# Block attention's step tables re-ordered, one convolution step moved, and the last unit's columns halved, in a one-core kernel of six mixer and feed-forward blocks

## The chip, the cores and the metric

The program runs on one core of a Trainium2 chip. The metric is the device time of one execution in microseconds (us), from launch to the output being written. Lower is better. Engines are named as in the profile: PE (TensorE), DVE (VectorE), ACT (ScalarE), POOL (GpSimd) and SP (SyncE, which here only issues transfers).

## The reference

A token block of 256 x 1024 in float32 passes through gated linear attention, feed-forward, a gated embedding, differential attention, feed-forward and gated embedding again, then a short convolution mixer and a block attention mixer. Only the last two and the end are touched by most of the change:

```python
# short convolution: h = h + (...)
b_gate, c_gate, xv, z = jnp.split(h @ w_in, 4, axis=-1)
u = c_gate * xv
conv = conv_w[0] * u_pad[:, 0:S] + ...            # three taps
y = b_gate * conv * jax.nn.silu(z);  return y @ w_out
# block attention, 16 heads of 64, one block of 256 keys, causal, with a distance bias
q, k, v, z = jnp.split(h @ w_in, 4, axis=-1)      # q, k normalised per head
s_own = q @ k.T - slope * own_dist                # masked above the diagonal
p = softmax(s_own);  out = p @ v
y = out * jax.nn.silu(z);  return y @ w_out
```

(The quoted lines are abridged.) In differential attention each head has two score maps, and the second, times a factor, is taken from the first before the product with v.

## The kernel before

**Units.** All weights are streamed once, in 297 units of 256 rows x 512 columns (512 KB each). A unit is fetched by SP into `raw` (a ring of four buffers), split by ACT into a rounded high part `whi` (L650) and by DVE into the rest, `wlo` (L1058; rings of eight). PE then runs 12 matmuls of 128x512 for it (L1773): two token halves, two halves of the unit's rows, and the three terms high x high, low x high, high x low. A tile is 512 output columns; most have four units. In block attention (`MB_IN` is unit 257, called M+0 here) tiles 0 to 7 are M+0 to M+31, and the output product is M+32 to M+39, which is unit 296, the last one.

**Order.** Each engine runs its own instruction list in order. What lies between the units (transposes, scores, softmax, products with v) is placed by hand in the tables `DF_ORDER` (differential attention) and `MB_ORDER` (block attention). An entry `(u, step, arg)` of PE's table is run ahead of unit M+u. ACT and DVE first split the weights up to some six units past u (`split_to`), and then run the step. SP's table says when it starts the two halves of a head's round trip: `out` writes the transposed probabilities of head `arg` to DRAM (`mb_blocks`, 192 KB), and `in` reads them back with their 32x32 blocks exchanged (`mb_pT`). Ahead of an entry at u, SP fetches all units up to M+u+9. The fetch of unit n waits until DVE has split unit n-4, whose buffer it takes:

```python
def fetch(lo, hi):
    for n in range(lo, hi):
        sp.wait_ge(sem("w_lo"), max(n - RAW + 1, 2))
        sp.dma_start(raw[:, n % RAW, :], stream[SOURCE[n]])...
```

**Block attention's steps.** `mb_T` (step `qkT`) transposes a tile of queries or keys for eight heads into banks 4 and 5, four transposes each. `mb_scores(i)` does two heads, mostly into banks 4 and 5. DVE's `mb_max(hd)` adds the bias (which frees the bank) and finds the row maximum. ACT's `mb_exp(hd)` follows. Heads 0 to 7 then go through DVE's block transpose `mb_blocks(hd)` (L1656; it writes one of two buffers, and from head 2 on waits until the `out` of head hd-2 has landed) and SP's round trip. Heads 8 to 15 are transposed by PE (`pT`, L2195). `mb_av(i)` is the product with v of heads 2i and 2i+1; for i = 1 it waits for `in` of heads 2 and 3, for i = 3 for heads 6 and 7. `mb_zn(g)` scales the gates of four heads by the softmax sums (L1666); `mb_zT(g)` transposes them into bank 4 or 5 (L2229), `mb_y(g)` multiplies them with the attention's output and frees that bank.

**Convolution.** `conv_parts(t, blk, at)` on DVE first splits the weights up to `at` + 6, then runs seven steps (L1590 to L1599), of which the sixth, `y_hi` (L1598), is what PE waits for ahead of a unit of the output product.

**End.** The last unit runs its six matmuls for the first token half, then six for the second; DVE adds each half to `h` (L1711), and SP writes it out (L573).

Of the kernel before, what the change touches and what calls it, by code (L numbers as in the profile page):

```python
# [83 lines left out]
def plan(first, tiles, steps, ends_first=False):  # L84
# [36 lines left out]
        (1, "second", 0), (8, "qkT", 0), (11, "qkT", 1), (12, "qkT", 2), (13, "scores", 0), (13, "qkT", 3),  # L121
# [7 lines left out]
        (13, "qkT", 3), (14, "scores", 0), (15, "scores", 1), (16, "tile", 3), (16, "aT", 0), (16, "scores", 2),  # L129
# [49 lines left out]
        (19, "sums", 3), (20, "max", 7), (20, "blk", 5), (21, "blk", 6), (22, "unit", 3), (25, "max", 8),  # L179
        (25, "blk", 7), (25, "max", 9), (27, "max", 10), (27, "max", 11), (29, "zn", 0), (29, "max", 12),  # L180
        (30, "max", 13), (31, "max", 14), (31, "max", 15), (31, "zn", 1), (31, "y", 0), (31, "ylo", 0),
        (31, "y", 1), (32, "zn", 2), (32, "zn", 3), (33, "ylo", 1), (33, "y", 2), (33, "ylo", 2), (34, "y", 3),
# [61 lines left out]
def build(nc, stream, x, p, cols_d, rows_d, consts_d, wgate_d, out):  # L244
    ctx = ExitStack()
    with ctx:
# [168 lines left out]
        def _(sp):  # L415
# [633 lines left out]
        def _(dve):  # L1049
# [570 lines left out]
            conv_parts(CV_IN + 7, 7, END[CV_OUT] + 1, last=True)  # L1620
# [95 lines left out]
        def _(pe):  # L1716
# [10 lines left out]
            def product(tile, lhs, signal, kt0=0, need=None, hooks=(), beside=None, part=None,  # L1727
# [10 lines left out]
                for k in range(n) if only is None else (only,):  # L1738
# [21 lines left out]
                    if turned:  # L1760
                        turned_unit(u, pair, k, kt0 + 2 * k, lhs, upper, fresh, n, inside)
                        continue
                    order = [(t, kk, i) for t in range(TT) for kk in range(2) for i in range(3)]
                    if u != UNITS - 1:
                        order.sort(key=lambda x: x[2])
                    for turn, (t, kk, i) in enumerate(order):
                        a, w = terms[i]
                        if turn == (1 if u == UNITS - 1 else 4):
# [4 lines left out]
                        last = T.matmul(bank[pair + t][:, :],  # L1773
                                        lhs[a][:, kt, t * P:(t + 1) * P],
                                        w[:, u % RING, kk * NW:(kk + 1) * NW],
                                        start=part != 1 and k == kk == i == 0,
                                        stop=part != 0 and k == n - 1 and kk == 1 and i == 2)
                        if u == UNITS - 1 and kk == 1 and i == 2:
                            last.then_inc(sem("last"), 1)
                    if u != UNITS - 1:  # L1780
                        last.then_inc(sem("w_used"), 1)
# [562 lines left out]
```

## Time and profile before

| | us |
|---|---|
| median of 3 runs (lowest, highest) | 904.68 (902.65, 905.58) |
| the profiled execution | 904.63 |
| its span, first to last instruction | 902.5 |
| PE busy | 893.9 |
| DVE busy | 654.6 |
| ACT busy | 508.1 |
| POOL busy | 55.2 |

The profiled execution's own time is 2.1 us longer than its span. Busy times are of the whole span, and a matmul's record overlaps the next one's, so PE's busy time says that it hardly ever ran dry, not how fast it was.

### The profile page before, as it was taken

To read this page: it belongs to the slowest core of one execution; us is meant where nothing else is said; L and a number is where in the kernel's file an instruction comes from. 1 tells how busy PE (TensorE), PEld (TensorE's weight loads), DVE (VectorE), ACT (ScalarE), POOL (GpSimd) and SP (SyncE) were. 2 spreads that over 40 slices of the span, in tenths; PEclk is the share of its full clock that TensorE was granted. 3 is DMA by queue.
4 is the path that set the end of the run, shared out by engine and by line. 5 is a ranking of instruction groups with operands and counts; after the bars stand their busy time and mean duration, and the time that the engine had idled before them with its cause. 6 is when DMAs were issued, how large, how long until landed. Compare 5 with 4: busy or idle time off the path is not lost.

```text
span 902.5 us, 12222 instructions
## 1 busy us (share of the span) xinstructions
PE 893.9 (99%) x4358; PEld 736.8 (82%) x4358; DVE 654.6 (73%) x995; ACT 508.1 (56%) x821; POOL 55.2 (6%) x59
## 2 busy tenths in 40 slices
PE   9999999999999999999999999999999999999998
PEld 8988888888888888778888888888888888887776
DVE  6985488777736699997787666646678898689663
ACT  6756554444444667788564444435664545486681
POOL 0001000000000003111100000000010000312000
PEclk9999999999999999999999999999999999999999
DMA  7564459777756666523487777746557775657711
GB/s 270 197 230 158 153 200 312 258 243 236 242 186 209 210 214 203 166 84 127 147 299 250 240 250 242 248 147 228 208 208 268 251 262 188 228 187 217 237 57 47
DMA packets 81197, 187.47 MB, mean 208 GB/s; under 512 B 10933, under 2 KB 36661, under 8 KB 81145
## 3 DMA queue, kind: packets, MB, share of 16 engines
q1 hardware_dynamic: 80712, 186.14, 61.8%
q8 instruction: 31, 0.51, 0.2%
q10 hardware_dynamic: 432, 0.66, 0.2%
q14 instruction: 22, 0.17, 0.1%
HBM read 171.83 MB, written 14.94 MB: 207 GB/s over the span
## 4 chain that ended last, share of the span: by engine, by line
PE 81%; DVE 10%; DMA 4%; issue 3%; ACT 2%; DVEq 0%; SPq 0%; ACTq 0%
PE bank L1773 70%; DVE wlo L1058 4%; DMA raw<-stream_dram 3%; PE bank L1800 3%; PE bank L1815 1%; PE bank L2101 1%; PE bank L2185 1%; DVE cv_prod L1557 1%; DMA cv_blocks<-cv_blk 1%; PE bank L2075 1%; ACT whi L650 1%; PE bank L2214 0%; PE bank L1858 0%; PE bank L2171 0%; DVE df_m L1463 0%
## 5 line engine op out<-in xcount | busy, mean ns | idle before, releaser
L650 ACT ACTIVATE whi<-raw 128x1024 fp32r<-128x1024 f32 x295 | 306.5, 1060 | 192.1 <-DMA raw<-stream_dram 116.5
L1058 DVE TENSOR_TENSOR wlo<-raw,whi 128x1024 fp32r<-128x1024 f32 x295 | 347.9, 1214 | 55.7 <-ACT whi L650 55.0
L1773 PE MATMUL bank<-whi,x_hi 128*128 128x512 f32 x560 | 152.5, 394 | 0.0
L1773 PE MATMUL bank<-wlo,x_hi 128*128 128x512 f32 x560 | 149.9, 389 | 0.0
L1773 PE MATMUL bank<-whi,x_lo 128*128 128x512 f32 x560 | 149.8, 389 | 0.0
L1773 PEld LDWEIGHTS bank<-wlo,x_hi 128*128 128x128 f32 x560 | 105.1, 188 | 22.2
L1773 PEld LDWEIGHTS bank<-whi,x_lo 128*128 128x128 f32 x560 | 105.1, 188 | 22.0
L1773 PEld LDWEIGHTS bank<-whi,x_hi 128*128 128x128 f32 x560 | 103.4, 188 | 21.8 <-issue 1.0
L1773 PE MATMUL bank<-whi,y_hi 128*128 128x512 f32 x400 | 109.7, 395 | 0.5 <-DVE y_hi L1598 0.3
L1773 PE MATMUL bank<-wlo,y_hi 128*128 128x512 f32 x400 | 107.6, 389 | 0.0
L1773 PE MATMUL bank<-whi,y_lo 128*128 128x512 f32 x400 | 107.6, 389 | 0.0
L1773 PEld LDWEIGHTS bank<-wlo,y_hi 128*128 128x128 f32 x400 | 75.1, 188 | 15.9
L1773 PEld LDWEIGHTS bank<-whi,y_lo 128*128 128x128 f32 x400 | 75.1, 188 | 15.9
L1773 PEld LDWEIGHTS bank<-whi,y_hi 128*128 128x128 f32 x400 | 73.5, 188 | 16.8 <-issue 1.0
L803 ACT ACTIVATE ffn_silu<-bank,rstd 128x256 f32<-128x256 f32 x44 | 18.5, 472 | 79.1 <-PE bank L1773 79.1
L1282 DVE SCALAR_TENSOR_TENSOR ffn_mid<-bank,rstd,ffn_silu 128x256 f32<-128x256 f32 x44 | 19.3, 479 | 55.4 <-ACT ffn_silu L803 55.4
L1773 PE MATMUL bank<-whi,mid_hi 128*128 128x512 f32 x176 | 47.0, 389 | 0.0
L1773 PE MATMUL bank<-wlo,mid_hi 128*128 128x512 f32 x176 | 47.0, 389 | 0.0
L1773 PE MATMUL bank<-whi,mid_lo 128*128 128x512 f32 x176 | 47.0, 389 | 0.0
L1088 DVE TENSOR_TENSOR h<-h,bank 128x512 f32<-128x512 f32 x22 | 14.1, 684 | 44.1 <-PE bank L1773 43.9
L1773 PEld LDWEIGHTS bank<-wlo,mid_hi 128*128 128x128 f32 x176 | 33.0, 188 | 6.9
L1773 PEld LDWEIGHTS bank<-whi,mid_lo 128*128 128x128 f32 x176 | 33.0, 188 | 6.9
(242 smaller groups left out, 847.8 us busy)
## 6 DMA issues: line engine op xcount, KB each, us to landing
raw<-stream_dram SPq DMA_DIRECT2D x295, 512.0 KB, 4.6
ffn_blocks<-ffn_blk SPq DMA_DIRECT2D x22, 256.0 KB, 2.0
ffn_land<-ffn_blocks SPq DMA_DIRECT2D x22, 256.0 KB, 4.0
second_blocks<-h_blk SPq DMA_DIRECT2D x8, 256.0 KB, 2.0
h_land<-second_blocks SPq DMA_DIRECT2D x8, 256.0 KB, 3.3
cv_blocks<-cv_blk SPq DMA_DIRECT2D x7, 256.0 KB, 5.6
cv_land<-cv_blocks SPq DMA_DIRECT2D x7, 256.0 KB, 2.8
h_blocks<-h_blk SPq DMA_DIRECT2D x3, 512.0 KB, 6.4
```

What stands on the lines that cost most here:

```text
L650: A(whi[:, u % RING, :], raw[:, u % RAW, :], ACT.Copy).then_inc(sem("w_hi"), 1)
L803: A(sg[:, (t - tin) % 2, k, :], bank[2 * (t % 2) + k][:, 0:256], ACT.Silu, scale=rstd[:, j, k:k + 1]).then_inc(sem("ffn_silu"), 1)
L1058: V.tensor_tensor(wlo[:, u % RING, :], raw[:, u % RAW, :], whi[:, u % RING, :].bitcast(F32), ALU.subtract).then_inc(sem("w_lo"), 1)
L1088: V.tensor_tensor(h[:, t, half * HALF:(half + 1) * HALF], h[:, t, half * HALF:(half + 1) * HALF], bank[2 * (tile % 2) + t][:, :], ALU.add) ...
L1282: V.scalar_tensor_tensor(mid[:, (t - tin) % 2, :, k, :], bank[2 * (t % 2) + k][:, 256:512].rearrange("p (k n) -> p k n", k=2), rstd[:, j, ...
L1557: last = V.scalar_tensor_tensor(cprod[:, (t - CV_IN) % 2, m, k, :], src, rstd[:, 6, k:k + 1], cact[:, (t - CV_IN) % 2, k, m, :], ALU.mult, ...
L1773: last = T.matmul(bank[pair + t][:, :], lhs[a][:, kt, t * P:(t + 1) * P], w[:, u % RING, kk * NW:(kk + 1) * NW], start=part != 1 and k == ...
L1800: last = T.matmul(bank[pair + hd // 2][:, hd % 2 * SEQ:(hd % 2 + 1) * SEQ], w[:, u % RING, kk * NW + hd * P:kk * NW + (hd + 1) * P], lhs[a ...
L1815: last = T.transpose(bank[b][:, k * SEQ + t * P:k * SEQ + (t + 1) * P], src[:, t, kt * P:(kt + 1) * P], ident)
L2075: last = T.matmul(bank[DF_S_BANKS[hd][m]][:, q * SEQ:(q + 1) * SEQ], dT[r, 0, hd, q * P:(q + 1) * P], dT[r, 1, hd, :], start=True, stop=True)
L2101: last = T.matmul(bank[b][:, q * SEQ + (hd % 2) * P:q * SEQ + (hd % 2 + 1) * P], daT[:, hd % 4, k * SEQ + q * P:k * SEQ + (q + 1) * P], dv ...
L2185: last = T.matmul(bank[MB_S_BANKS[i][m]][:, (0, P)[q]:(P, 3 * P)[q]], mT[r, 0, i, q * P:(q + 1) * P], mT[r, 1, i, 0:(q + 1) * P], start=Tr ...
```

## The change

Four things are changed. (1) Table entries of differential attention: `qkT` 2 and 3 run together ahead of `scores` 0 at +13, and ACT runs `exp` of head 1 one entry earlier. (2) In block attention's tables `max` 7, `exp` 7 and the copy of `qkT` 2 move up, `av` 2 moves from +25 to +27, `zn` 0 and 1 (and on PE `zT` 0 and 1) run together ahead of the last `scores`, 7, and SP's round trips take later places among the weights. (3) The last `conv_parts` runs ahead of one split. (4) The last unit works in three pieces: the first token half whole, then two column halves of the second one in two banks of their own, whose earlier sum is added to `h` beforehand.

```diff
+LAST = ((0, 0, NW), (1, 0, NW // 2), (1, NW // 2, NW))
...
     "sp": (
-        (12, "out", 0), (14, "in", 0), (15, "out", 1), (17, "in", 1), (17, "out", 2), (17, "out", 3), (17, "in", 2),
...
+        (14, "out", 0), (15, "out", 1), (15, "in", 0), (17, "out", 2), (17, "in", 1), (18, "out", 3), (18, "out", 4),
...
-            for half in range(2):
-                for t in range(TT):
-
-                    sp.wait_ge(sem("h_new"), 28 + 2 * half + t + 1)
-                    sp.dma_start(out[t * P:(t + 1) * P, half * HALF:(half + 1) * HALF],
-                                 h[:, t, half * HALF:(half + 1) * HALF]).then_inc(sem("out_done"), 16)
-            sp.wait_ge(sem("out_done"), 64)
+            for t in range(TT):
+                sp.wait_ge(sem("h_new"), 28 + t + 1)
+                sp.dma_start(out[t * P:(t + 1) * P, 0:HALF], h[:, t, 0:HALF]).then_inc(sem("out_done"), 16)
+            for n, (t, lo, hi) in enumerate(LAST):
+                sp.wait_ge(sem("h_new"), 30 + n + 1)
+                sp.dma_start(out[t * P:(t + 1) * P, HALF + lo:HALF + hi], h[:, t, HALF + lo:HALF + hi])\
+                    .then_inc(sem("out_done"), 16)
+            sp.wait_ge(sem("out_done"), 16 * (TT + len(LAST)))
...
-            conv_parts(CV_IN + 7, 7, END[CV_OUT] + 1, last=True)
+            conv_parts(CV_IN + 7, 7, END[CV_OUT], last=True)
...
-            for t in range(TT):
-                dve.wait_ge(sem("last"), t + 1)
-                V.tensor_tensor(h[:, t, HALF:], h[:, t, HALF:], bank[2 * ((MB_OUT + 3) % 2) + t][:, :], ALU.add)\
-                    .then_inc(sem("h_new"), 1)
+            pair = 2 * ((MB_OUT + 3) % 2)
+            dve.wait_ge(sem("w_used"), UNITS - 1)
+            V.tensor_tensor(h[:, 1, HALF:], h[:, 1, HALF:], bank[pair + 1][:, :], ALU.add).then_inc(sem("h_part"), 1)
+            dve.wait_ge(sem("h_part"), 1)
+            for n, (t, lo, hi) in enumerate(LAST):
+                b = pair if t == 0 else (pair + 2) % 4 + n - 1
+                dve.wait_ge(sem("last"), n + 1)
+                V.tensor_tensor(h[:, t, HALF + lo:HALF + hi], h[:, t, HALF + lo:HALF + hi], bank[b][:, 0:hi - lo],
+                                ALU.add).then_inc(sem("h_new"), 1)
...
+            def last_unit(u, pair, k, kt, lhs, n):
+
+                c.wait(pe, "w_lo", u + 1)
+                for m, (t, lo, hi) in enumerate(LAST):
+                    b = pair if t == 0 else (pair + 2) % 4 + m - 1
+                    if t:
+                        claim(b)
+                    for kk in range(2):
+                        for i, a, w in ((0, 0, whi), (1, 0, wlo), (2, 1, whi)):
+                            last = T.matmul(bank[b][:, 0:hi - lo], lhs[a][:, kt + kk, t * P:(t + 1) * P],
+                                            w[:, u % RING, kk * NW + lo:kk * NW + hi],
+                                            start=t == 1 and kk == i == 0, stop=kk == 1 and i == 2)
+                    last.then_inc(sem("last"), 1)
```

**SP, the round trips of heads 0 to 3.** Before, from the fetch of M+8 on (a `raw` row is one unit, an `mb_blocks` row an `out`, an `mb_pT` row an `in`):

```order
L441 DMA raw<-stream_dram 128x1024 [waits w_lo] x14
L560 DMA mb_blocks<-p_tok 128x384 [waits mb_blk]
L441 DMA raw<-stream_dram 128x1024 [waits w_lo] x2
L565 DMA mb_pT<-mb_blocks 128x4x96 [waits mb_out0]
L441 DMA raw<-stream_dram 128x1024 [waits w_lo]
L560 DMA mb_blocks<-p_tok 128x384 [waits mb_blk]
L441 DMA raw<-stream_dram 128x1024 [waits w_lo] x2
L565 DMA mb_pT<-mb_blocks 128x4x96 [waits mb_out1]
L560 DMA mb_blocks<-p_tok 128x384 [waits mb_blk] x2
L565 DMA mb_pT<-mb_blocks 128x4x96 [waits mb_out0]
L441 DMA raw<-stream_dram 128x1024 [waits w_lo]
L565 DMA mb_pT<-mb_blocks 128x4x96 [waits mb_out1]
```

The same stretch in the changed kernel:

```order
L442 DMA raw<-stream_dram 128x1024 [waits w_lo] x16
L561 DMA mb_blocks<-p_tok 128x384 [waits mb_blk]
L442 DMA raw<-stream_dram 128x1024 [waits w_lo]
L561 DMA mb_blocks<-p_tok 128x384 [waits mb_blk]
L566 DMA mb_pT<-mb_blocks 128x4x96 [waits mb_out0]
L442 DMA raw<-stream_dram 128x1024 [waits w_lo] x2
L561 DMA mb_blocks<-p_tok 128x384 [waits mb_blk]
L566 DMA mb_pT<-mb_blocks 128x4x96 [waits mb_out1]
L442 DMA raw<-stream_dram 128x1024 [waits w_lo]
L561 DMA mb_blocks<-p_tok 128x384 [waits mb_blk] x2
L442 DMA raw<-stream_dram 128x1024 [waits w_lo]
L566 DMA mb_pT<-mb_blocks 128x4x96 [waits mb_out0]
```

The `out` of head 0 now stands behind units 279 and 280 (which before followed it), and the `in` of head 2 behind the fetches of units 284 and 285, where it stood ahead of both. The next two rows of the changed list are the fetch of unit 286 and the `in` of head 3, which before stood ahead of unit 285.

**DVE, maximum of head 7.** Before, after the unit-long step on `mb_tok` (`unit` 2); the four rows from L1640 to L1648 are one head's maximum:

```order
L1446 TENSOR_TENSOR mb_tok<-mb_tok,mb_ss 128x512 x2
L1640 SCALAR_TENSOR_TENSOR mb_s<-consts,bank 128x384
L1644 TENSOR_REDUCE mb_stat<-mb_s 128x1
L1645 TENSOR_REDUCE mb_stat<-mb_s 128x1
L1648 TENSOR_SCALAR mb_stat<-mb_stat 128x2
L1058 TENSOR_TENSOR wlo<-raw,whi 128x1024
L1439 TENSOR_REDUCE mb_ss<-mb_sq 128x8 x2
L1058 TENSOR_TENSOR wlo<-raw,whi 128x1024
L1640 SCALAR_TENSOR_TENSOR mb_s<-consts,bank 128x384
```

In the changed kernel:

```order
L1448 TENSOR_TENSOR mb_tok<-mb_tok,mb_ss 128x512 x2
L1642 SCALAR_TENSOR_TENSOR mb_s<-consts,bank 128x384
L1646 TENSOR_REDUCE mb_stat<-mb_s 128x1
L1647 TENSOR_REDUCE mb_stat<-mb_s 128x1
L1650 TENSOR_SCALAR mb_stat<-mb_stat 128x2
L1642 SCALAR_TENSOR_TENSOR mb_s<-consts,bank 128x384
L1646 TENSOR_REDUCE mb_stat<-mb_s 128x1
L1647 TENSOR_REDUCE mb_stat<-mb_s 128x1
L1650 TENSOR_SCALAR mb_stat<-mb_stat 128x2
L1060 TENSOR_TENSOR wlo<-raw,whi 128x1024
L1441 TENSOR_REDUCE mb_ss<-mb_sq 128x8 x2
L1060 TENSOR_TENSOR wlo<-raw,whi 128x1024
```

Head 7's maximum now stands ahead of the splits of units 281 and 282.

**PE, ahead of M+31.** Before (L2185 scores 7, L2195 transposes of probabilities, L2214 products with v, L2229 gates):

```order
L2185 MATMUL bank<-mb_qkT 128x128 x2
L2185 MATMUL bank<-mb_qkT 128x256 x2
L2195 MATMUL bank<-consts,mb_p 128x128 x3
L2214 MATMUL bank<-mb_pT,mb_v 64x256 x2
L2214 MATMUL bank<-mb_pT,mb_v 64x128 x2
L2214 MATMUL bank<-mb_pT,mb_v 64x256 x2
L2214 MATMUL bank<-mb_pT,mb_v 64x128 x2
L2195 MATMUL bank<-consts,mb_p 128x128 x3
L2229 MATMUL bank<-consts,mb_z 128x128 x8
L2195 MATMUL bank<-consts,mb_p 128x128 x3
```

In the changed kernel:

```order
L2249 MATMUL bank<-consts,mb_z 128x128 x8
L2215 MATMUL bank<-consts,mb_p 128x128 x3
L2234 MATMUL bank<-mb_pT,mb_v 64x256 x2
L2234 MATMUL bank<-mb_pT,mb_v 64x128 x2
L2234 MATMUL bank<-mb_pT,mb_v 64x256 x2
L2234 MATMUL bank<-mb_pT,mb_v 64x128 x2
L2215 MATMUL bank<-consts,mb_p 128x128 x3
L2205 MATMUL bank<-mb_qkT 128x128 x2
L2205 MATMUL bank<-mb_qkT 128x256 x2
L2215 MATMUL bank<-consts,mb_p 128x128 x3
```

The gates' transposes and the last scores have changed places.

## Rows read from the trace of the kernel before

**Rows 1.** Page, part 1: busy time, share of the span, instructions.

```profile
PE 893.9 (99%) x4358; PEld 736.8 (82%) x4358; DVE 654.6 (73%) x995; ACT 508.1 (56%) x821; POOL 55.2 (6%) x59
```

**Rows 2.** Waits of PE: who waited for whom: us in total, times, longest.

```profile
PE bank L2229 <- DVE mb_z L1666: 1.4, 1, 1.4
...
PE bank L2171 <- ACT mb_qkT L990: 0.8, 1, 0.8
PE bank L2171 <- DVE mb_s L1640: 0.6, 1, 0.6
PE bank L1773 <- DVE y_hi L1598: 0.3, 1, 0.3
PE bank L2075 <- ACT df_qkT L885: 0.2, 1, 0.2
PE bank L2061 <- issue: 0.2, 1, 0.2
PE bank L1773 <- ACT df_p L898: 0.2, 1, 0.2
```

**Rows 3.** Timeline of PE, 828.5 to 856: start us, us, line, op, count.

```profile
829.08 0.60 PE L2171 MATMUL bank<-consts,mb_tok 128*128 128x128 f32 x4
830.25 0.66 PE L2171 MATMUL bank<-consts,mb_tok 128*128 128x128 f32 x4 [0.58 <-DVE mb_s L1640]
830.84 1.52 PE L2214 MATMUL bank<-mb_pT,mb_v 128*64 128x256 f32 x16
832.29 1.21 PE L1773 MATMUL bank<-whi,x_hi 128*128 128x512 f32 x4
...
843.68 0.93 PE L2185 MATMUL bank<-mb_qkT 64*128 64x128 f32 x8
...
854.31 0.87 PE L2214 MATMUL bank<-mb_pT,mb_v 128*64 128x256 f32 x8
```

**Rows 4.** Timeline of SP's issues, 806 to 825.

```profile
806.79 0.33 SPq L560 DMA_DIRECT2D mb_blocks<-p_tok  x1
807.16 2.37 SPq L441 DMA_DIRECT2D raw<-stream_dram  x2
...
824.15 0.43 SPq L565 DMA_DIRECT2D mb_pT<-mb_blocks  x1
```

**Rows 5.** Timeline of DVE, 810 to 850.

```profile
810.97 0.86 DVE L1656 STREAM_TRANSPOSE p_tok<-mb_p 128x384 f32<-128x384 f32 x1
...
817.06 0.56 DVE L1640 SCALAR_TENSOR_TENSOR mb_s<-consts,bank 128x384 f32<-128x384 f32 x1 [0.47 <-PE bank L2185]
...
821.77 0.87 DVE L1656 STREAM_TRANSPOSE p_tok<-mb_p 128x384 f32<-128x384 f32 x1 [1.19 <-ACT mb_p L1001]
...
828.52 1.22 DVE L1058 TENSOR_TENSOR wlo<-raw,whi 128x1024 fp32r<-128x1024 f32 x1
...
844.60 0.55 DVE L1640 SCALAR_TENSOR_TENSOR mb_s<-consts,bank 128x384 f32<-128x384 f32 x1 [3.07 <-PE bank L2185]
...
847.97 2.35 DVE L1058 TENSOR_TENSOR wlo<-raw,whi 128x1024 fp32r<-128x1024 f32 x2
```

**Rows 6.** DMA issues at 806.79, 824.15 and 831.80: count, KB, us to landing.

```profile
mb_blocks<-p_tok SPq DMA_DIRECT2D x1, 192.0 KB, 1.9
...
mb_pT<-mb_blocks SPq DMA_DIRECT2D x1, 192.0 KB, 3.9
...
mb_pT<-mb_blocks SPq DMA_DIRECT2D x1, 192.0 KB, 2.6
```

**Rows 7.** Timeline of DVE, 884 to 900, and the output's DMA issues (last row).

```profile
884.28 0.74 DVE L1681 TENSOR_TENSOR mb_oT<-bank,mb_sq 128x256 f32<-128x256 f32 x2
...
899.33 0.69 DVE L1711 TENSOR_TENSOR h<-h,bank 128x512 f32<-128x512 f32 x1 [0.67 <-PE bank L1773]
...
out<-h SPq DMA_DIRECT2D x4, 256.0 KB, 2.1
```

**Rows 8.** Timeline of PE at its start: four transposes of 128x128.

```profile
4.89 1.09 PE L1815 MATMUL bank<-consts,h 128*128 128x128 f32 x4
```

More of the change, by code:

```diff
@@ L120 @@
     "pe": (
-        (1, "second", 0), (8, "qkT", 0), (11, "qkT", 1), (12, "qkT", 2), (13, "scores", 0), (13, "qkT", 3),
+        (1, "second", 0), (8, "qkT", 0), (11, "qkT", 1), (13, "qkT", 2), (13, "qkT", 3), (13, "scores", 0),
         (13, "scores", 1), (16, "scores", 2), (16, "aT", 0), (17, "qkT", 4), (18, "aT", 1), (18, "scores", 3),
@@ L128 @@
         (4, "tile", 0), (8, "tile", 1), (9, "qkT", 0), (12, "qkT", 1), (12, "tile", 2), (12, "qkT", 2),
-        (13, "qkT", 3), (14, "scores", 0), (15, "scores", 1), (16, "tile", 3), (16, "aT", 0), (16, "scores", 2),
+        (12, "qkT", 3), (14, "scores", 0), (14, "scores", 1), (16, "tile", 3), (16, "aT", 0), (16, "scores", 2),
         (17, "qkT", 4), (17, "aT", 1), (18, "scores", 3), (18, "qkT", 5), (19, "qkT", 6), (19, "qkT", 7),
@@ L160 @@
         (11, "qkT", 0), (12, "qkT", 1), (13, "scores", 0), (13, "scores", 1), (18, "scores", 2), (19, "scores", 3),
[5 rows of a table removed]
+        (22, "qkT", 2), (22, "av", 0), (22, "av", 1), (24, "qkT", 3), (25, "scores", 4), (27, "scores", 5),
[4 rows of a table added]
     "act": (
@@ L168 @@
         (14, "exp", 1), (15, "exp", 2), (16, "tile", 3), (16, "exp", 3), (16, "exp", 4), (18, "exp", 5),
-        (20, "tile", 4), (20, "exp", 6), (22, "oT", 0), (23, "exp", 7), (23, "qkT", 2), (24, "tile", 5),
+        (20, "tile", 4), (20, "exp", 6), (20, "exp", 7), (22, "qkT", 2), (22, "oT", 0), (24, "tile", 5),
         (25, "qkT", 3), (25, "exp", 8), (26, "exp", 9), (26, "pT", 8), (27, "exp", 10), (28, "tile", 6),
-        (28, "pT", 9), (29, "oT", 1), (29, "exp", 11), (30, "pT", 10), (30, "exp", 12), (30, "pT", 11),
-        (30, "exp", 13), (31, "pT", 12), (31, "exp", 14), (31, "oT", 2), (32, "yhi", 0), (32, "pT", 13),
-        (32, "tile", 7), (32, "exp", 15), (32, "yhi", 1), (32, "pT", 14), (33, "pT", 15), (34, "yhi", 2),
+        (28, "pT", 9), (29, "oT", 1), (29, "exp", 11), (30, "pT", 10), (30, "exp", 12), (30, "exp", 13),
+        (31, "pT", 11), (31, "yhi", 0), (31, "pT", 12), (31, "oT", 2), (31, "exp", 14), (32, "pT", 13),
+        (32, "exp", 15), (32, "tile", 7), (32, "yhi", 1), (32, "pT", 14), (33, "pT", 15), (34, "yhi", 2),
         (35, "zT", 3), (36, "yhi", 3),),
@@ L178 @@
         (17, "max", 4), (17, "max", 5), (17, "blk", 3), (17, "blk", 4), (18, "unit", 2), (18, "max", 6),
[L179 to L182, printed above, removed]
+        (18, "max", 7), (19, "sums", 3), (20, "blk", 5), (21, "blk", 6), (22, "unit", 3), (25, "max", 8),
+        (25, "blk", 7), (25, "max", 9), (27, "max", 10), (27, "max", 11), (29, "zn", 0), (29, "zn", 1),
+        (29, "max", 12), (30, "max", 13), (31, "y", 0), (31, "y", 1), (31, "max", 14), (31, "max", 15),
+        (31, "ylo", 0), (32, "zn", 2), (32, "zn", 3), (33, "ylo", 1), (33, "y", 2), (33, "ylo", 2), (34, "y", 3),
         (35, "ylo", 3),),
     "sp": (
-        (12, "out", 0), (14, "in", 0), (15, "out", 1), (17, "in", 1), (17, "out", 2), (17, "out", 3), (17, "in", 2),
-        (18, "in", 3), (18, "out", 4), (19, "in", 4), (20, "out", 5), (21, "in", 5), (22, "out", 6), (23, "in", 6),
-        (23, "out", 7), (24, "in", 7),),
+        (14, "out", 0), (15, "out", 1), (15, "in", 0), (17, "out", 2), (17, "in", 1), (18, "out", 3), (18, "out", 4),
+        (19, "in", 2), (20, "in", 3), (21, "out", 5), (22, "out", 6), (23, "in", 4), (23, "in", 5), (24, "in", 6),
+        (26, "out", 7), (27, "in", 7),),
 }
@@ L1762, in product @@
                         continue
+                    if u == UNITS - 1:
+                        last_unit(u, pair, k, kt0 + 2 * k, lhs, n)
+                        continue
                     order = [(t, kk, i) for t in range(TT) for kk in range(2) for i in range(3)]
-                    if u != UNITS - 1:
-                        order.sort(key=lambda x: x[2])
+                    order.sort(key=lambda x: x[2])
                     for turn, (t, kk, i) in enumerate(order):
                         a, w = terms[i]
-                        if turn == (1 if u == UNITS - 1 else 4):
+                        if turn == 4:
                             c.wait(pe, "w_lo", u + 1)
@@ L1776, in product @@
                                         start=part != 1 and k == kk == i == 0,
[L1777 to L1781, printed above, removed]
+                                        stop=part != 0 and kk == 1 and i == 2 and (k == n - 1 or (u == UNITS - 2 and t == 1)))
+                    last.then_inc(sem("w_used"), 1)
                 if signal is not None:
```

9 rows, old and new, of the table MB_ORDER are left out of this document.

## The prediction

> **What bounds the kernel now.** I read the page's busy times first. PE is busy for 99% of the span and DVE, the next one, for 73% [rows 1], so time is won only where PE stands still and lost only where it is made to. PE's waits come next. Among them seven lie where the change works, and they sum to 1.4 + 0.8 + 0.6 + 0.3 + 0.2 + 0.2 + 0.2 = 3.7 us [rows 2]. The listed length is a little short, because a matmul's record runs on past the start of the next one. Four transposes that start at 829.08 have a record of 0.60 us, so they start some 0.11 apart and the fifth was due at about 829.52. It started at 830.25, which is 0.73 late, where the row says 0.58 [rows 3]. I add 0.15 to each wait: 3.7 + 7 x 0.15 = 4.75 us is all that the changed tables can win back. Last come the timelines of PE, SP and DVE around M+22, the place at which PE first needs round trips [rows 3 to 5], and how long such transfers take [rows 6].
>
> **Differential attention.** `qkT` 3 directly behind `qkT` 2 takes away the wait of L2075 for the copy, and `exp` 1 one entry earlier takes away the wait of L1773 for `df_p` and the idle time of L2061: 3 x (0.2 + 0.15), with the unrounded sizes nearer 0.93. Now `scores` 0 comes after them, and it waits until ACT has copied `qkT` 2. No row shows that wait. It is at least nothing (the four transposes of `qkT` 3 cover 0.44 us of it), and at most about the 0.8 + 0.15 that PE waits for ACT's copy in block attention [rows 2]. I take the middle, 0.48. Net: **-0.45**, between -0.9 and 0.
>
> **Convolution.** The last `conv_parts` runs one split earlier. A split holds DVE for 1.22 us (its row) and the next work starts 1.13 after it [rows 5], more than the 0.3 + 0.15 that PE waits for `y_hi` [rows 2]. So that wait goes: **-0.42**. The split that is now behind makes one weight fetch about 3 us later, and weights arrive some units ahead of PE there. If that cover were gone it would cost up to 1 us.
>
> **End.** The last add is of 256 columns. Two adds of 128x256 take 0.74 with one record's overlap, about 0.41 each, against 0.69 for 512: -0.28. The last output transfer is 128 KB in place of 256 KB, of which each took 2.1 [rows 7]. I take -0.25 for it, between 0 (the time is all fixed) and -1.0 (it is all bytes). Twelve matmuls of 256 columns in place of six of 512 cost at most 12 x 0.02, and I take 0.08. The extra add of 0.69 lies beside the first half's six matmuls, four of which alone last 1.21 [rows 3]. If it did not, it would cost its 0.69. Net: **-0.45**, between -1.2 and +0.3.
>
> **Block attention, what is removed.** `max` 7 and with it bank 5 are free before `qkT` 2 gets there: -0.73. `exp` 7 and the copy of `qkT` 2 come earlier, which ends the 0.8 + 0.15 of L2171: -0.95. The gates are transposed ahead of the last scores, when nobody else uses their banks, so that L2229 does not wait: -1.55. The costs of both moves lie under DVE's and ACT's idle time, 3.07 us of it at 844.60 alone [rows 5].
>
> **Block attention, first new wait.** In the old order SP issued `out` 0 at 806.79, then two fetches, the second of them at about 807.16 + 2.37 - 0.33 = 809.2 [rows 4]. Now `out` 0 is issued behind that second one, at about 809.57, and it is queued behind its 512 KB. It landed after 1.9 us when alone. A round trip's transfer behind a fetch took 3.9 [rows 6], so I take 813.4. DVE's third block transpose starts at 810.97 in the old order [rows 5], writes the buffer that `out` 0 reads, and must wait for the landing: it stands for 2.4 us. Behind it on DVE are splits, maxima and the next transposes. DVE catches up 0.47 at 817.06 and most of 1.19 at 821.77 [rows 5]. (The latter is called a wait for ACT, but `out` 2, issued at 817.81, landed just before, and it is issued at nearly the same time as before.) DVE stays about 0.8 late, between 0 and 2.4.
>
> Next, `max` 7 stands ahead of the splits of units 281 and 282. One maximum is 1.3 us: from 844.60 to 847.97 there are two and a block transpose of 0.8 [rows 5]. The split of unit 282 starts at 828.52 and lasts 1.22 [rows 5], so it now ends at 829.7 + 1.3 + 0.8 = 831.8. The fetch of unit 286 waits for it. `in` of head 3, which before went out at 824.15 [rows 4], now stands behind that fetch: it is issued at about 832.3, and with 3.9 [rows 6] it lands at **836.2**.
>
> PE needs heads 2 and 3 for `av` 1. Without any wait it starts `qkT` 2 at 829.08, needs 0.9 for eight transposes and 0.7 for `av` 0 (half of 1.52), and is at `av` 1 at 830.7. It waits **5.5 us**. `av` 1 takes 0.7, and unit 279 starts at 836.9 to 837.0 in place of 832.29 [rows 3]: +4.7, in which the 0.73 that was won is already counted. With DVE not late and the fetch of 286 at 830.0, `in` 3 goes out at 830.3 and lands at 834.2: the wait is 3.5 and the loss +2.6. Splits do not run dry in the meantime: PE stands, and they go on.
>
> **Block attention, second new wait.** `out` 7 now stands behind the fetch of unit 292, which waits for the split of unit 288. From `scores` 4 (843.68) DVE does max 8, the transpose of head 7 and max 9, and then two splits from 847.97, of which the first is unit 288's and ends at about 849.1: 5.4 after `scores` 4. Issue at 5.8, landing with 3.9, and then `in` 7 with 2.6, what one took with no fetch close ahead [rows 4 to 6]: 12.3. PE reached `av` 3 10.6 after `scores` 4 (854.31 - 843.68 [rows 3]), and `av` 2 now lies between, 0.7 more: 11.3. It waits 1.0 to 1.1, between 0 and 2.5 if the last transfer takes 3.9 as well. Block attention's sum: +4.7 - 0.95 + 1.05 - 1.55 = **+3.2**.
>
> **Sum.** The profiled execution took 904.63, its span 902.5 and 2.1 around it; the median of the runs is 904.68, so no correction is due. 904.63 - 0.45 - 0.42 - 0.45 + 3.2 = **906.5 us**.
>
> **The clock.** PE's longest listed wait of all was 1.4 us [rows 2], and the page shows the granted clock at its upper level throughout. At the start, after no work, four transposes took 1.09 [rows 8], against 0.60 for four at 829.08 [rows 3]; by their starts that is half speed, 1.2 in place of 2.4 GHz, and work of 4 to 5 us was done so, at a price of about half of that. A wait of 5.5 us has no like in this trace, so whether the clock falls in it is open: 0 if not, up to 2.4 if it falls at once, and some 2 us if late in the wait. The Trainium skill, "TensorE: Matmul & The Clock Gate", Part 1: The HAM clock gate, says that an engine that idles is put back to half clock and gets full speed again after sustained work. By that rule the time is 908.5 if the wait counts as idling; the start of this trace agrees with it, the middle does not test it.
>
> **Rivals.**
> (A) The wait is there, and the clock holds: 906.5. Chance 0.36.
> (B) The wait is there, and the clock falls: 906.5 + 2.0 = 908.5. Chance 0.28. For it: the start's half speed. Against: no fall in the old trace, with waits up to 1.4.
> (C) The wait is short. DVE catches up wholly, since 0.47 + 1.19 of idle time and SP's own slack may be worth more than I count: 906.5 - 2.1 = 904.4. Chance 0.16.
> (D) The other side: `in` 3 is in time. It decides at the split of unit 282. If that ends before about 826.4, `in` 3 is issued at 826.8 and lands by 830.7, so that PE never waits. Then all listed waits go: 904.63 - 0.73 - 0.95 - 1.55 - 0.45 - 0.42 - 0.45 = 900.1. For it: the round trips of heads 0 and 1 have much room. Against: in the old order, with no `max` 7 ahead, that split ended only at 829.7 [rows 5]; transfers of 2.6 would not be enough either. Chance 0.11.
> (E) Worse: `out` 0 needs longer behind two fetches, DVE is 2.4 late, and `in` 3 lands at 838. Or the clock falls twice: 909 or more. Chance 0.09.
>
> **How the numbers follow.** The likeliest is A, 906.5, with its own range of 905 to 908 (the bounds of the two waits' transfers, and of the small terms). C, A and B lie in 902 to 909.5, with some of D's near edge; left out are D's rest and most of E, 2 in 10. A measurement of this kernel can tell 0.3%, 2.7 us, from no change: faster is below 902.0, slower above 907.4. Faster: D and a corner of C, 0.13. Slower: B for the most part, E and the upper end of A, 0.39. Same: 0.48.
>
> **What the profile after would show.** Of the first new wait: PE waits at L2234 (products with v) for a transfer of `mb_pT`, 5 to 6 us around 831, once, and SP issues `in` 3 right behind a fetch at about 832; DVE idles 2.4 us ahead of its third block transpose. Of the second: about 1 us at L2234 ahead of the last `scores` but one. Gone are the waits of L2191 for `mb_s` and `mb_qkT`, of L2249 for `mb_z`, and of L1782 for `y_hi`; in differential attention a wait for `df_qkT` of 0.3 to 0.5 stays, now at the scores. Last add 0.41. Of the clock: the column of the slice behind 836 shows under full speed, or not. The prediction is wrong if no L2234 wait is there (D), or if it is nearer to 3 (DVE absorbed the delay) or 8 us.

## The result, and the profile after

The changed kernel takes **908.89 us** (median of 6 runs, 908.5 to 910.56). The kernel before took 905.08 in the runs on the same chip (6 runs, 902.62 to 905.85). The ratio is **1.0049, 95% interval 1.0036 to 1.0061**: slower by about 4.4 us (3.8 by the two medians). The profiled execution took 908.7 us with a span of 906.7, against 904.63 and 902.5 before. The comparison is thus a span that is 4.2 us longer.

First the page's busy times, as in [rows 1], of the changed kernel:

```profile
PE 896.2 (99%) x4364; PEld 740.4 (82%) x4364; DVE 655.3 (72%) x997; ACT 507.3 (56%) x820; POOL 54.0 (6%) x59
```

They say nearly nothing: the six matmuls and two DVE instructions more are those of the last unit's pieces. PE's waits, as in [rows 2], do:

```profile
PE bank L2234 <- DMA mb_pT<-mb_blocks: 3.6, 2, 2.2
PE bank L2205 <- DVE mb_s L1642: 1.6, 1, 1.6
...
PE bank L2106 <- DVE df_p L1505: 0.6, 1, 0.6
PE bank L2095 <- ACT df_qkT L887: 0.5, 2, 0.2
```

The waits for `mb_z`, `mb_qkT`, `mb_s` ahead of `qkT` 2, and `y_hi` are gone, as the change intended (`mb_z` holds the gates). In their place stand two waits at L2234, the products with v, for a round trip, and one of 1.6 us at L2205, the scores. The timeline of PE, as in [rows 3], shows where:

```profile
820.85 0.93 PE L2205 MATMUL bank<-mb_qkT 64*128 64x128 f32 x8 [1.63 <-DVE mb_s L1642]
821.70 1.51 PE L1782 MATMUL bank<-whi,x_hi 128*128 128x512 f32 x4
823.01 1.91 PE L1782 MATMUL bank<-wlo,x_hi 128*128 128x512 f32 x4
...
831.61 1.03 PE L2191 MATMUL bank<-consts,mb_tok 128*128 128x128 f32 x8
832.58 0.87 PE L2234 MATMUL bank<-mb_pT,mb_v 128*64 128x256 f32 x8
835.66 1.21 PE L2234 MATMUL bank<-mb_pT,mb_v 128*64 128x256 f32 x8 [2.21 <-DMA mb_pT<-mb_blocks]
836.80 2.08 PE L1782 MATMUL bank<-whi,x_hi 128*128 128x512 f32 x4
...
860.22 0.87 PE L2234 MATMUL bank<-mb_pT,mb_v 128*64 128x256 f32 x8 [1.34 <-DMA mb_pT<-mb_blocks]
```

The eight transposes at 831.61 run with no wait between them. `av` 1 waits at 835.66, `av` 3 at 860.22. Two groups of four matmuls of 128x512 are slow, 1.91 and 2.08 us in place of 1.1. The table of stretches of 2 us says why (start and end, length, busy time of each engine, then the granted clock, the DMA share and GB/s):

```profile
822.00:824.00 2.00, 2.00 (x7) 1.52 (x6) 2.00 (x3) 2.00 (x7) 0.00 (x0) 0.60 0.03 7
824.00:826.00 2.00, 2.00 (x7) 1.58 (x6) 1.97 (x5) 1.92 (x3) 0.00 (x0) 0.55 0.34 68
...
836.00:838.00 2.00, 2.00 (x11) 1.33 (x8) 1.66 (x2) 1.09 (x2) 0.00 (x0) 0.51 0.91 297
838.00:840.00 2.00, 2.00 (x8) 1.57 (x7) 1.23 (x1) 0.45 (x1) 0.00 (x0) 0.63 0.95 338
```

The granted clock (the third number from the right) falls to the lower level (1.2 GHz) behind each of the first two waits. In stretches of 0.1 us it is there from 822.4 to 825.9 and from 836.0 to 839.4, 3.4 us each time. SP's issues, as in [rows 4], and DVE's timeline, as in [rows 5], show the cause of the waits:

```profile
808.88 0.33 SPq L442 DMA_DIRECT2D raw<-stream_dram  x1
809.26 1.66 SPq L561 DMA_DIRECT2D mb_blocks<-p_tok  x1
...
831.58 0.33 SPq L442 DMA_DIRECT2D raw<-stream_dram  x1
831.96 0.43 SPq L566 DMA_DIRECT2D mb_pT<-mb_blocks  x1
...
853.32 0.43 SPq L561 DMA_DIRECT2D mb_blocks<-p_tok  x1
854.07 0.33 SPq L442 DMA_DIRECT2D raw<-stream_dram  x1
857.15 0.38 SPq L566 DMA_DIRECT2D mb_pT<-mb_blocks  x1
```

```profile
813.31 0.85 DVE L1658 STREAM_TRANSPOSE p_tok<-mb_p 128x384 f32<-128x384 f32 x1 [2.55 <-DMA mb_blocks<-p_tok]
...
830.34 1.22 DVE L1060 TENSOR_TENSOR wlo<-raw,whi 128x1024 fp32r<-128x1024 f32 x1
```

`out` 0 at 809.26 stands behind a weight fetch and holds DVE for 2.55 us. The split of unit 282 starts at 830.34 where it started at 828.52. The fetch of unit 286 follows it at 831.58, and `in` 3 follows the fetch at 831.96. The landings of `out` 0 and of `in` 3 took, as in [rows 6]:

```profile
mb_blocks<-p_tok SPq DMA_DIRECT2D x1, 192.0 KB, 4.0
...
mb_pT<-mb_blocks SPq DMA_DIRECT2D x1, 192.0 KB, 3.7
```

At the end, DVE's last adds and the output's last transfers, as in [rows 7]:

```profile
902.69 1.06 DVE L1718 TENSOR_TENSOR h<-h,bank 128x512 f32<-128x512 f32 x2 [0.74 <-PE bank L1801]
904.05 0.42 DVE L1718 TENSOR_TENSOR h<-h,bank 128x256 f32<-128x256 f32 x1 [0.30 <-PE bank L1801]
```

```profile
out<-h SPq DMA_DIRECT2D x2, 128.0 KB, 1.9
```

The first matmul of the last unit starts 5.64 us before the end of the span (901.06 of 906.7), before 6.09 (896.41 of 902.5).

### The profile page after: what moved, and what is told of

It reads as the page before. It is cut to its first block, busy times and chain, and to the rows that moved or that the text cites. A ratio compares the mean times of both kernels' runs of the same rounds, so it can differ in the third digit from the quotient of the medians.

```text
span 906.7 us, 12238 instructions
## 1 busy us (share of the span) xinstructions
PE 896.2 (99%) x4364; PEld 740.4 (82%) x4364; DVE 655.3 (72%) x997; ACT 507.3 (56%) x820; POOL 54.0 (6%) x59
## 4 chain that ended last, share of the span: by engine, by line
PE 86%; DVE 8%; DMA 3%; issue 1%; ACT 1%; POOL 0%; SPq 0%; DVEq 0%; ACTq 0%
PE bank L1782 75%; DVE wlo L1060 4%; PE bank L1820 3%; DMA mb_blocks<-p_tok 1%; PE bank L1835 1%; DMA raw<-stream_dram 1%; PE bank L2121 1%; DMA mb_pT<-mb_blocks 1%; PE bank L2095 1%; PE bank L2234 1%; DVE df_m L1465 0%; DVE df_tok L1469 0%; PE bank L1878 0%; DVE df_stat L1489 0%; PE bank L2106 0%
```

## The experiments

The theory was that SP's new table makes the loss, through the queue: a transfer behind a fetch, the fetch behind a split, the split behind a DVE instruction that waits for another transfer. The main rival was that the moved maxima, gates and copies cost something themselves. All ratios are against the kernel before, in runs on the same chip.

### e1: out 0 early

```diff
-        (14, "out", 0), (15, "out", 1), (15, "in", 0), ...
+        (12, "out", 0), (15, "out", 1), (15, "in", 0), ...
```

> The changed kernel with one entry of SP's table put back: the out of head 0 at +12, ahead of two weight fetches, in place of +14. Theory (queue): DVE's 2.55 us wait ahead of its third block transpose goes, with it PE's 1.63 at scores 3 and the half clock of 822 to 826 (1.6 us). But PE then comes 3.3 us earlier to av 1, and in of head 3 hardly moves (about 0.5 earlier, still behind the fetch of unit 286), so the wait at L2234 grows from 2.2 to about 5 us and swallows it: about 908.4 in all, between 907 and 909. Rival (waits add up): what goes here is won, 3.3 us: 905.6.

Measured: 906.55 us, ratio 1.0014 (0.9998 to 1.0030). The median lies between the two expectations. The wait at scores 3 and the half clock there are gone, and the wait at `av` 1 grew from 2.2 to 3.0, where 5 was expected:

```profile
829.26 0.87 PE L2234 MATMUL bank<-mb_pT,mb_v 128*64 128x256 f32 x8
833.12 1.55 PE L2234 MATMUL bank<-mb_pT,mb_v 128*64 128x256 f32 x8 [2.99 <-DMA mb_pT<-mb_blocks]
834.59 2.08 PE L1782 MATMUL bank<-whi,x_hi 128*128 128x512 f32 x4
```

Against the changed kernel this is 1.7 us less by the differences of the medians (2.1 and 3.8 above the kernel before) and 3.2 by the ratios, which is too wide to say how near it comes to the rival's 3.3. The traces say where it comes from. Unit 279 starts at 834.59 in place of 836.80, because `in` 3 is issued at 829.54 in place of 831.96 and lands at 833.1: the releaser of the second wait moved, which the theory had put at 0.5 us. DVE's timeline shows why. The split of unit 282 started at 827.91, 2.4 us earlier than in the changed kernel:

```profile
818.91 1.81 DVE L1658 STREAM_TRANSPOSE p_tok<-mb_p 128x384 f32<-128x384 f32 x2
...
827.91 1.22 DVE L1060 TENSOR_TENSOR wlo<-raw,whi 128x1024 fp32r<-128x1024 f32 x1
```

The transposes of heads 3 and 4 follow one another (x2, one record of 1.81 us), where the kernel before stood still for 1.19 us between them [rows 5]. SP's new table puts `out` 2 ahead of `in` 1, and it went out at 814.76 in place of 817.81 (before; 818.01 in the changed kernel). The new table thus also gives DVE something, which the forecast had left out.

### e2: in 2 and in 3 ahead of the fetches

```diff
-        ... (17, "in", 1), (18, "out", 3), (18, "out", 4),
-        (19, "in", 2), (20, "in", 3), (21, "out", 5), ...
+        ... (17, "in", 1), (18, "out", 3), (18, "in", 2),
+        (18, "in", 3), (18, "out", 4), (21, "out", 5), ...
```

> The changed kernel with in of heads 2 and 3 put ahead of the fetches of units 285 and 286 (and ahead of out of head 4). Theory (queue): the scores 3 wait and its half clock stay (3.3 us), the L2234 wait around 833 goes, and with it its half clock: 2.2 + 1.6 less, 905.0, between 904 and 906.5. Rival (DVE is simply late, whatever the queue): in 3 still lands after PE wants it, and the time stays at 908 to 909.

Measured: 903.63 us, ratio 0.9983 (0.9969 to 0.9998). The queue theory's range was missed low by 0.4 us and its rival by 4 and more. The wait at `av` 1 and the half clock behind it are gone; scores 3 waited 2.5 us in the profiled execution, with half clock from 820.7 to 827.5, and `av` 3 less than a microsecond. That execution took 905.90, the slowest of the ten, and is not typical. The theory had taken the fall behind scores 3 as certain; the mean granted clock was 1.000 in seven of the ten runs (902.40 to 904.02), and 0.996 to 0.998 in the other three (903.93 to 905.90). PE's waits in the profiled execution:

```profile
PE bank L2205 <- DVE mb_s L1642: 2.5, 1, 2.5
...
PE bank L2234 <- DMA mb_pT<-mb_blocks: 0.8, 1, 0.8
```

### e3: both

> Both edits of SP's table together. Theory (queue): neither wait, no half clock around 822 to 840; of the new waits only the one at av 3 (1.3 us) is left, and all the old ones that the change removes are gone: 901.3, between 900 and 902.5. Waits in series at one place then show as: e1 alone wins 0.5, e2 alone 3.9, both 7.6. Rival (the loss lies in the moved maxima and gates of the other engines): over 904.

Measured: 901.81 us, ratio 0.9969 (0.9954 to 0.9984). With both edits the changed kernel takes less than the kernel before (2.8 us by the ratio), and the rival falls. PE's waits:

```profile
PE bank L2205 <- ACT mb_qkT L992: 1.5, 1, 1.5
...
PE bank L2234 <- DMA mb_pT<-mb_blocks: 0.9, 1, 0.9
```

The second is the expected one at `av` 3. The first was not expected: scores 4 waits for ACT's copy of `qkT` 3.

### e4: SP's new table alone, in the kernel before

> The kernel before with nothing but SP's new table for block attention. Theory (queue): the table alone makes the loss, larger than the whole change does, since no old wait is won back: scores 3 about 1.7 and its half clock 1.6, av 1 about 1 to 2, av 3 about 1.7, less the 0.7 of bank 5 that is hidden: 910.4, between 908.5 and 912. Rival (the loss lies elsewhere): 904 to 906.

Measured: 909.1 us, ratio 1.0046 (1.0028 to 1.0064). The table alone makes a loss as large as the whole change does. It is within the range but 1.3 below the 910.4 that was expected; the profiled execution took 910.70, and so it cannot say why the median is lower. Behind its wait at scores 3, 1.82 us long, the clock did not fall; in the next, 2.91 us long, it did (half clock from 833.4 to 840.3):

```profile
820.59 0.93 PE L2185 MATMUL bank<-mb_qkT 64*128 64x128 f32 x8 [1.82 <-DVE mb_s L1640]
...
834.82 1.55 PE L2214 MATMUL bank<-mb_pT,mb_v 128*64 128x256 f32 x8 [2.91 <-DMA mb_pT<-mb_blocks]
836.29 2.08 PE L1773 MATMUL bank<-whi,x_hi 128*128 128x512 f32 x4
```

The rest of the change, which the forecast counted at -4.6 us, hardly shows on top of the table: the ratio is 1.0046 with the table alone and 1.0049 with all, and the profiled execution with all is 2.0 us shorter (908.7 for 910.7). Part of the reason is in PE's waits of this run. Those for the copy of `qkT` 2 and for bank 5 are gone here too, since PE comes there later; of the old waits of block attention only the gates' 1.4 us is left to win. And one part of the rest adds to the loss: here, with `max` 7 still behind it, the split of unit 282 starts at 828.72, and `in` 3 is issued at 830.34 and lands at 834.8, where the changed kernel has 830.34, 831.96 and 835.6. That `max` 7 (1.3 us) accounts for this is read from DVE's order; no run moves it alone.

### e5: SP's old table, all else changed

The three lines of `"sp"` in `MB_ORDER` are those of the kernel before.

> The changed kernel with SP's table for block attention wholly as it was before. Theory (queue): all three new waits of PE go (scores 3, av 1, av 3) and the rest of the change wins what the forecast counted, some 4.6 us: about 900.3 in all, between 899.5 and 902. Rival (the other tables cost something of their own): 903 or more.

Measured: 905.04 us, ratio 0.9999 (0.9985 to 1.0013). **The expectation was wrong by 4.7 us.** The three waits at scores 3, `av` 1 and `av` 3 went, but another took their place:

```profile
842.78 1.65 PE L2205 MATMUL bank<-mb_qkT 64*128 64x128 f32 x8 [2.75 <-ACT mb_qkT L992]
```

It is the wait that e3 showed, 2.75 us long, and the eight matmuls behind it take 1.65 in place of 0.93, at half clock. ACT's timeline gives its chain, with SP's ahead of it:

```profile
836.62 1.06 ACT L652 ACTIVATE whi<-raw 128x1024 fp32r<-128x1024 f32 x1 [1.11 <-DMA raw<-stream_dram]
837.59 1.25 ACT L718 ACTIVATE mb_v<-bank,rstd 128x512 f32<-128x512 f32 x2
840.42 1.06 ACT L652 ACTIVATE whi<-raw 128x1024 fp32r<-128x1024 f32 x1 [1.59 <-DMA raw<-stream_dram]
841.39 1.25 ACT L992 ACTIVATE mb_qkT<-bank,mb_gain 128x512 f32<-128x512 f32 x2
```

```profile
835.00 0.37 SPq L566 DMA_DIRECT2D mb_pT<-mb_blocks  x1
835.41 0.50 SPq L442 DMA_DIRECT2D raw<-stream_dram  x1
```

The fetch at 835.41 is unit 288's. It stood behind `in` 5, which waited for its `out` to land (issued at 831.26, 3.7 us), and it landed at 840.40, 5.0 us after its issue. ACT splits that unit at 840.42, and the copy of `qkT` 3, ready in the bank since 837.3 (PE's transposes start at 836.25 and last 1.03), stands behind the split in ACT's list. The old kernel did not show this, because PE came there some 2.8 us later and had `av` 2 ahead of scores 4: the copy ended at 843.5, and scores 4 started at 843.68. It had no room to spare. So the old waits that the other tables remove are gone here, and what they win is given back at scores 4.

### e6: block attention's tables as before

> The changed kernel with all of block attention's tables as before: only the differential attention entries, the convolution step and the end are left of the change. By the traces so far the end is worth 0.45, differential attention 0.2 to 0.4, and the convolution step 0 to 0.4 (the wait that it takes away was there in one execution of two): 0.7 to 1.2 less than before, 903.5, ratio 0.999. Rival (the forecast's terms as they stand): 1.3 less.

Measured: 903.23 us, ratio 0.9987 (0.9978 to 0.9996), 1.2 us less than before by the ratio, between 0.4 and 2.0. Both expectations, 0.7 to 1.2 and 1.3, lie within it; the runs do not tell them apart.

### e7: scores 3 one unit later

```diff
-        ... (18, "scores", 2), (19, "scores", 3),
+        ... (18, "scores", 2), (20, "scores", 3),
```

> The changed kernel with PE's scores 3 one unit later (+20 in place of +19), so that a unit of matmuls fills the 1.63 us for which PE stood there. Theory (waits at one place in series): no wait and no half clock around 822, but DVE is as late as before and in of head 3 lands at the same time (835.6), so PE waits about 5 us at L2234 in place of 2.2; the clock falls there again, for as long or longer: 908.9, between 908 and 910. Rival (waits add up): 905.6. On the clock: if the half-clock stretch after a wait of 5 us costs the same 1.6 to 2 us as after 2.2, its price does not grow with the wait.

Measured: 908.92 us, ratio 1.0044 (1.0028 to 1.0059), as the theory had it and 3.3 above the rival. The wait at scores 3 is gone, and nothing is won, since PE waits that much longer for the same transfer:

```profile
829.21 0.87 PE L2234 MATMUL bank<-mb_pT,mb_v 128*64 128x256 f32 x8
835.97 1.55 PE L2234 MATMUL bank<-mb_pT,mb_v 128*64 128x256 f32 x8 [5.89 <-DMA mb_pT<-mb_blocks]
837.44 2.08 PE L1782 MATMUL bank<-whi,x_hi 128*128 128x512 f32 x4
```

The clock fell at 834.1, within the wait, and was back at 840.9. That stretch at half clock, 6.8 us, is as long as those around the waits of 2.5 to 3.0 us in e1, e2, e4 and e5, and twice as long as the one at the wait of 2.21 us of the changed kernel.

### e8 to e10: the copy of qkT 3, and the best version

e8 takes e3's table, with

```diff
# act
-        (25, "qkT", 3), (25, "exp", 8), ...
+        (24, "qkT", 3), (25, "exp", 8), ...
# sp
-        (26, "out", 7), (27, "in", 7),
+        (25, "out", 7), (26, "in", 7),
```

> The version with both edits of SP's table (out 0 early, in 2 and 3 ahead of the fetches), and two more: out 7 and in 7 one entry earlier (+25, +26), and ACT's copy of qkT 3 ahead of the splits that wait for weights (+24). Theory: the two waits that were left there, 1.5 us at scores 4 for ACT's copy and 0.9 at av 3 for a transfer, go as well: 901.8 - 2.4 = 899.4, between 898.5 and 901. Rival (the copy only delays the splits, and PE waits for those instead): 901 to 902.

Measured: **900.28 us, ratio 0.9950 (0.9937 to 0.9964)**. Both waits went: scores 4 and both products with v run without one.

e9 puts only the copy at +24, under SP's old table:

> The changed kernel with SP's old table (as e5) and ACT's copy of qkT 3 one entry earlier (+24), ahead of two splits, of which the second waited for a weight fetch in e5. Theory (ACT's list stands behind a late fetch): PE's 2.75 us at scores 4 and the half clock behind it (2.1) go: 905.0 - 4.8 = 900.3, between 899.5 and 901.5, which is what the forecast gave for the change with no new wait. Rival (the copy is bounded by PE or the bank, not by the fetch): 903 or more.

Measured: **899.87 us, ratio 0.9949 (0.9931 to 0.9966)**. One entry of ACT's table is worth about 5 us here: 5.2 by the medians (905.04 to 899.87, on two chips), 4.5 by the ratios. Not all of it is the wait. The three runs of e5 whose mean granted clock was 1.000 took 901.64 to 902.59, some 2 to 3 us more than e9; the rest of the 5 us goes with the half clock of the other seven. What is left at scores 4 is 0.4 us:

```profile
PE bank L2205 <- ACT mb_qkT L992: 0.4, 1, 0.4
```

e10 has e8's copy, but `out` 7 and `in` 7 where the change put them:

> As e3 (out 0 early, in 2 and 3 ahead of the fetches) with ACT's copy of qkT 3 at +24, but out 7 and in 7 where the change put them. It separates the two edits that e8 adds to e3. Theory: the copy's 1.5 us are won, the 0.9 at av 3 stay or grow by what PE comes earlier: 900.3 to 901.3; e8 had 900.28.

Measured: 900.58 us, ratio 0.9960 (0.9946 to 0.9974). The wait at `av` 3 is there, 0.9 us. Against e3 (0.9969) and e8 (0.9950) the intervals overlap, so the split of the last 1.5 us between the two edits rests on the traces alone.

### e11: av 1 later

```diff
# pe
-        (22, "av", 0), (22, "av", 1), (24, "qkT", 3), ...
+        (22, "av", 0), (24, "av", 1), (24, "qkT", 3), ...
# act
-        (22, "oT", 0), (24, "tile", 5),
+        (24, "oT", 0), (24, "tile", 5),
```

> The changed kernel with PE's av 1 (and ACT's copy oT 0 that follows it) at +24 in place of +22: the consumer is moved, not the transfer. Theory: in of head 3 still lands at about 835.6, while PE works on two units until about 838; the 2.2 us of L2234 and the half clock behind them (1.6) go, the 3.3 at scores 3 and the 1.3 at av 3 stay: 908.9 - 3.8 = 905.1, between 904 and 906.5. Rival (something else comes last there: the copy of qkT 3 or a weight): 907 or more.

Measured: 904.15 us, ratio 0.9998 (0.9987 to 1.0009), within the expected range, but partly by luck, since its parts are not the expected ones: `av` 1 and `av` 3 do not wait, scores 3 waits 1.6 without a half clock behind it, and scores 4 waits again for the copy:

```profile
843.98 0.93 PE L2205 MATMUL bank<-mb_qkT 64*128 64x128 f32 x8 [1.76 <-ACT mb_qkT L992]
```

So moving the consumer takes away the wait at `av` 1 as moving the transfer does (e2, 0.9983; the intervals overlap).

## Why the prediction was partly wrong

The predicted time was 906.5, and 908.89 was measured: inside the range, but on the slower side of the bound of 2.7 us, to which 0.39 was given and 0.48 to no change. The forecast made the profiled execution 1.9 us longer, and its span became 4.2 us longer. **The step that failed is the clock, which the sum held up and so put at 0: it cost 1.5 us** (0.3 within `av` 1 and 1.2 in unit 279). Of the other 0.8, some 0.4 lies in the terms for differential attention and the convolution, which did not come out where they were counted, and 0.35 in a wait that the forecast does not have. The mechanism of the two new waits that it forecast was right; a third was missed. Point by point:

**First new wait: right in mechanism, place and end.** "It is issued at about 832.3, and with 3.9 [rows 6] it lands at **836.2**": it was issued at 831.96 and landed 3.7 later, at 835.6. "Unit 279 starts at 836.9 to 837.0": it started at 836.80. DVE's wait for `out` 0 was forecast as 2.4 and was 2.55, and DVE was 0.5 late at the split ahead of `max` 6 (823.03 for 822.57), where 0.8 was taken. e2 shows that the place of `in` 2 and 3 is what causes this. But the sum takes another 0.87 off for the gains of the earlier stages, which makes +3.8 at unit 279, and it was +4.5.

**What the delay of DVE meets on its way: missed.** The step "Behind it on DVE are splits, maxima and the next transposes" priced the delay only through the splits and took 0.47 of it as caught up at 817.06. That idle time is a wait for PE's scores 2. The reverse wait was not looked for: scores 3 needs the banks that DVE's late maxima free. PE waited 1.63 us there, with a half clock behind it that cost 1.6 (the unit that starts at 821.70 takes 4.4 us to the next, 826.14, against 2.86, 820.77 to 823.63, before). It did not change when unit 279 starts, because `in` 3 sets that, but for the same reason the wait at `av` 1 was 2.2 and not 5.5. The forecast's own sign of being wrong, a wait nearer to 3 us, came, and not for the reason that it gave (DVE absorbing the delay). e7 shows it: without the wait at scores 3 it is 5.89, and the time stays.

**The clock: the less likely of the two cases came.** The sum held the clock up (A, 0.36); the rival B (0.28) let it fall at a price of 2.0 and gave 908.5, which is 0.4 from the measured time. That nearness is partly luck: B's price was 0.5 too high, and the terms that both share were 0.8 too low. Unit 279 took 4.1 us (836.80 to 840.89) in place of 2.9 (832.29 to 835.18), so the fall cost 1.2 behind the wait itself, and some 0.3 within `av` 1 (1.14 us from its start to unit 279, in place of 0.80). The rule that B follows, that an engine which idles is put back to half clock, is that of the Trainium skill, "TensorE: Matmul & The Clock Gate", Part 1: The HAM clock gate. The trace agrees with it in direction: the clock was at its lower level from 836.0 on, behind a wait of 2.21 us. The error was to give the lower chance to the case that the start of the same trace had an example of, when a wait of 5.5 us had no example of a steady clock.

**Second new wait: right, a little small.** Forecast 1.0 to 1.1, listed 1.34 (with the 0.15 that the forecast adds to a listed wait, 1.5). Forecast 12.3 us from scores 4 to the landing of `in` 7; it landed 12.8 after (847.38 to 860.2, which is 857.15 + 3.0).

**What is removed: right for two of three.** The three waits of block attention are gone. The copy of `qkT` 2 was counted at -0.95 and gave -1.1, the gates at -1.55 and gave -1.6; the -0.73 at bank 5 cannot be read apart from the new wait. e9, which has none of the new waits, takes 899.87; the forecast's rival D, all won and nothing lost, gave 900.1, but for a kernel without e9's edit of ACT's table. One wait was not counted because the kernel before hid it: the copy of `qkT` 3 (e3, e5). D's statement that it needs only `in` 3 in time was wrong, since e5 has that and takes 905.04.

**The end: right.** -0.45 forecast, 6.09 - 5.64 = 0.45 in the profile: last add 0.42 (0.41 forecast), last transfer 1.9 for 128 KB against 2.1 for 256 KB. The Trainium skill, "DMA: Bandwidth & Descriptors", section "Anatomy of one DMA — SWDGE (gpsimd) path", gives most of a small transfer's time as fixed, for transfers that GpSimd issues. These are issued by SP, and the trace agrees with it for them too: half the bytes save 0.2 us.

**Differential attention and convolution: not shown as counted.** Forecast -0.45 and -0.42. The wait for `df_p` did not go but moved to L2106, 0.6 us in the listing above, which the forecast did not foresee; in the profiled executions of e1, e2, e3, e5 and e6 it was 0.3 to 0.5. The wait for `y_hi` was 0.3 in the profiled execution of before, and it is absent in that of e4, which has the old convolution code. So one execution's wait of 0.3 us was taken as the kernel's. e6 bounds the three together (with the end) at 0.4 to 2.0 us won. One execution per kernel cannot say more: e4 is the same program as before's up to block attention's round trips, and PE reaches scores 0 at 799.55 in its trace and at 800.77 in that of before.

In one line, by unit starts: +4.5 (unit 279, 836.80 against 832.29: the wait at `av` 1 and all that came before it) and +1.2 (clock) - 1.1 (copy of `qkT` 2) + 1.3 (second wait and the move of `av` 2) - 1.6 (gates) + 0.35 (a later start of the output product's second unit, 882.37, which the profile puts down to ACT) - 0.45 (end) = 4.2, the difference of the spans.

## What to carry to other kernels

A transfer's place in the queue fixes two times, its own and that of every fetch behind it, and in both directions an instruction that waits in order passes the delay on. When something is moved, follow its delay not only to who reads its result but also to who needs the buffer or bank that the waiting engine would have freed.

Waits at one place are in series: e7 removes the earlier one alone and wins nothing; e1 removes its cause and wins 2 to 3 us, because that cause also delayed the transfer which ends the later wait. Move the last releaser, and then look again, because a stall that goes uncovers the next (here the copy of `qkT` 3 behind a weight split, one table entry and about 5 us).

A wait of PE can cost more than its length when TensorE's clock falls in or behind it, here 1.5 to 2.9 us more. All waits of 2.2 us and more that were traced here had such a fall, so a forecast with a wait like that should take its price into the sum, and the steady clock as the other case.

## What the runs showed of the hardware

**The clock falls at some waits and not at others of nearly the same length.** At PE waits of 2.2 us and more it fell in each profiled execution here: 2.21 (after), 2.49 (e2), 2.75 (e5), 2.91 (e4), 2.99 (e1) and 5.89 (e7). Behind 1.51 (e3), 1.57 (e11) and 1.82 (e4) it did not, but behind 1.63 (after) and 1.76 (e11) it did. In the five longest it fell before the wait was over (in e7 at 834.1, 1.9 us before its end) and stayed at its lower level for 6.8 us; in the other three it fell 0.3 to 1.6 us after the wait's end, for 3.4 us. By the starts of the next unit each cost between 1.5 and 2.9 us beside the wait; the longest wait, 5.89, cost 2.3, and that of 2.49 cost 2.9. What decides it between 1.6 and 1.8 us stays open; no run here was made to find it.

**It also differs between runs of one kernel.** For e5 the mean granted clock over the span was 1.000 in three runs, and they took 901.64 to 902.59; it was 0.996 to 0.998 in seven, and they took 904.57 to 906.37. In e11 it is six runs of 902.65 to 904.16 against four of 905.19 to 906.20. In e4 it was 1.000 in two of ten, and these were no faster than the rest (908.87 and 908.98). In e3, e8, e9 and e10, in which PE has no wait in block attention above 1.51 us, it was 1.000 in all 25 runs. The kernel before has it too: beside e1 to e4 it was 0.998 in 5 of 31 runs, and they took 906.08 to 909.08. So a median of a kernel with such waits hangs on how often the fall comes. Whether the waits of the runs without a fall were as long is not known, since each kernel has one trace: at scores 3, with the same tables up to there, PE waited 1.57 (e11), 1.63 (after) and 2.49 us (e2). The Trainium skill, "TensorE: Matmul & The Clock Gate", Part 1: The HAM clock gate, says that the number of slow matmuls varies from run to run of the same kernel at its start; these runs show the like in the middle of a kernel.
